# The second attention's output product in split parts, handed over group by group, without the two stops around it

## The chip, the cores and the metric

The kernel runs on one core of one Trainium2 chip. The metric is device time in microseconds (us), the median of the runs; lower is better. Five engines work side by side and meet only at semaphores: TensorE (PE, matrix products; PEld its weight loads), VectorE (DVE), ScalarE (ACT), GpSimd (POOL) and SyncE (SP, which here only issues transfers). Each engine works its own queue strictly in order, so an instruction that waits holds up all that is queued behind it on that engine.

## What is computed

A macaron transformer block (FFN, a hybrid mixer with a recurrence and a windowed attention, FFN), then two layers of a second block. Layer 1, the last, is the one that matters here:

```python
def window_attention(hl, hc, w_qkv, q_g, k_g, sink, w_o, need_ctx_out):
    ...
    ob = lax.map(block, jnp.arange(n_blocks))
    yl = jnp.moveaxis(ob, 0, 1).reshape(B, L, Q_DIM) @ w_o
    ...
        xl = xl + g1_l * yl
        hl2 = modulate(rms_norm_2(xl, norm_ffn_g[layer]), sh2_l, sc2_l).reshape(B * L, D)
        ...
        if last:
            xl = xl + g2_l * hier_moe(hl2, *moe_args).reshape(B, L, D)
```

There are 512 tokens, 1024 features, 16 query heads of 64 over 4 key heads, query blocks of 128 that see the neighbouring blocks, 256 context tokens and a sink, and a layer of 32 experts with two chosen for each token.

## The kernel before

Everything is held transposed: features on the partitions (8 tiles `k` of 128), tokens along the row. The work is one hand-written program for each engine, and what sets the order around the change is the order in which each queue was written, with semaphores between them.

**The attention loop.** Layer 1's attention has 32 units `U` (a pair of heads by a block of 128 queries), eight groups `G` of four. Unit `U` passes: scores on PE (`att_scores`, lines 705 and 710), scaling, mask and row minimum on DVE (`att_stats`, lines 1807 to 1815; `s_evac` says that the scores' banks are free, `max_ready` that the minimum is there), exponentials on ACT (`att_exps`, line 1264), transposes on PE (`att_turns`, line 726) into banks 4 and 5, and copies out of them on ACT (`att_copies`, line 1277). The engines run a few units apart: in step `U` PE turns unit `U - 2` and then scores unit `U`; ACT copies unit `U - 2` and then takes the exponentials of unit `U - 1`; DVE has the stats of unit `U`. A unit has four key blocks in the first and last quarter of the loop, five in between.

Once in four steps comes a group's end: reciprocals of the sums on DVE (`att_recips`, line 1820), turned into rows and spread over the partitions by PE (`att_rows`, `att_spread`, lines 736 and 743), the values product on PE (`att_values`, line 758), the spread reciprocals copied by ACT (`att_spread`, line 1290, into `tmp`, announced by `rec_copied`), and last `att_outputs` on DVE (line 1827), which multiplies the product by them into `f` (the tile `ar_f`) and announces `o_evac`. In DVE's step of `U % 4 == 3` the stats of unit `U` stand ahead of `att_outputs` of group `U // 4 - 1`.

**The output product.** `dense("wo", ...)` (line 535) multiplies plain f32 weights with `f`, eight tiles of eight products; the chip does each f32 product in two passes, so the trace counts 128 of them. DVE adds each tile, times a gate, to the stream `lat` (`gated_add`, lines 2232 and 2234). The weights come in four chunks of 1 MB, two tiles each, into `slot[0]` and `slot[1]`; SP loads chunks 2 and 3 when tiles 1 and 3 are done.

**The stops.** `Phase.end` drains an engine and makes it wait until all four compute engines stand there too. One stop lies between the attention and the product, one between the product and the norm.

**The norm.** ACT squares the eight tiles of `lat` (`squares`, line 1127), PE sums them over the partitions with a matrix of ones (`norm_sum`, line 680, 16 passes), ACT takes the root (`std`, line 1158), DVE inverts and scales, and `moe_layer(1)` begins: routing, then the loop over the blocks of the experts, whose weights SP streams.

**Split products.** Elsewhere the kernel already uses `split_products` (lines 547 and 553): weight and input each as a high part rounded to fp32r and a low part that is the rest, and of the four products the three that count, each one pass. ACT makes a weight piece's high part (`high`, line 1179), DVE or POOL its low part (line 1644 on DVE).

## Time and profile before

| | us |
|---|---|
| median of 3 runs | 3299.66 |
| lowest, highest | 3296.21, 3300.25 |
| the profiled execution | 3297.93 |
| its span, first to last instruction | 3296.1 |
| mean granted TensorE clock, share of full | 0.926 |
| PE, DVE, ACT, POOL busy over the span | 2822.9, 1287.4, 803.2, 365.7 |

All times in the rows are from the profiled execution, counted from its first instruction. A PE row's duration runs to the end that the profile models, and passes overlap, so the pace of the products is read from the distance between starts.

### The profile page before, as it was taken

The page shows a single profiled execution, that of the slowest core. Times are in us where ns is not written, and L with a number is a line of the kernel's source. Part 1 is how long each engine was busy: PE and PEld are TensorE (multiplying, and loading weights), DVE is VectorE, ACT ScalarE, POOL GpSimd, SP SyncE. Part 2 cuts the span into 40 slices and gives each one's busy share as a digit, 9 for nine tenths or more (in the row PEclk, how much of TensorE's full clock was granted, in tenths as well). Part 3 has the DMA queues.
Part 4 walks back from the last instruction along what each step waited for, and adds up shares of the span by engine and source line. Part 5 has one row for each costly group of instructions (what it writes and reads, how often), then busy time and mean ns, then how long its engine had stood idle before and what let it go on. Part 6 is the DMA issues. An engine that isn't in the chain of part 4 may idle for free. (4 is left out here: it accounts for less than half of the span.)

```text
span 3296.1 us, 34963 instructions
## 1 busy us (share of the span) xinstructions
PE 2822.9 (86%) x12512; PEld 1821.9 (55%) x12512; DVE 1287.4 (39%) x1978; ACT 803.2 (24%) x1338; POOL 365.7 (11%) x484
## 2 busy tenths in 40 slices
PE   6999998999989998698868888885778887888886
PEld 4888766767868886585643333333554434333332
DVE  4776576454476765303221111113386422111112
ACT  3323235454332332222210000001326520000000
POOL 0111000000000111322101111111400001111110
PEclk9999989999999999799869989897789997999998
DMA  4666521112335665110428999995110044999997
GB/s 166 211 222 219 202 69 73 64 64 78 108 128 197 213 229 187 49 64 13 169 99 346 397 401 398 403 400 235 40 37 1 1 193 187 405 402 398 402 403 286
DMA packets 117476, 672.10 MB, mean 204 GB/s; under 512 B 16398, under 2 KB 20878, under 8 KB 51856
## 3 DMA queue, kind: packets, MB, share of 16 engines
q1 hardware_dynamic: 77456, 542.63, 42.5%
q0 software_dynamic: 33600, 104.90, 9.3%
q10 hardware_dynamic: 6336, 23.50, 1.9%
q8 instruction: 47, 0.77, 0.1%
q14 instruction: 37, 0.30, 0.0%
HBM read 685.37 MB, written 24.38 MB: 215 GB/s over the span
## 5 line engine op out<-in xcount | busy, mean ns | idle before, releaser
L841 PE MATMUL bank<-big 128*64 128x512 f32 x1008 | 471.0, 613 | 102.5 <-DMA big<-in_w 100.8
L844 PE MATMUL bank<-big 128*64 128x512 f32 x1008 | 473.1, 615 | 0.0
L1983 DVE TENSOR_TENSOR big<-big,bank 64x512 f32<-64x512 f32 x65 | 44.9, 691 | 905.9 <-ACT big L1325 905.9
L841 PEld LDWEIGHTS bank<-big 128*64 128x64 f32 x1008 | 135.4, 141 | 407.8 <-issue 405.6
L856 PE MATMUL bank<-big 128*64 128x512 f32 x1008 | 269.2, 683 | 43.1 <-DVE big L1987 43.1
L1691 DVE SCALAR_TENSOR_TENSOR tabs<-tabs,tmp 128x1024 f32<-128x1024 f32 x160 | 193.3, 1222 | 182.4 <-DMA tabs<-in_wm 182.2
L2346 POOL DMA_DIRECT2D tabs<-in_wm x160 | 84.7, 530 | 1196.1 <-DVE tabs L1691 755.9
L547 PE MATMUL bank<-act_low 128*128 128x512 f32 (+1 forms) x480 | 166.6, 363 | 48.5 <-POOL u_split L2331 25.5
L1179 ACT ACTIVATE w_high<-slot 128x1024 fp32r<-128x1024 f32 (+1 forms) x134 | 136.5, 1040 | 228.3 <-DMA slot<-in_w 101.4
L856 PEld LDWEIGHTS bank<-big 128*64 128x64 f32 x1008 | 78.4, 155 | 186.9 <-issue 185.5
L1325 ACT ACTIVATE big<-bank 64x512 f32<-64x512 f32 x65 | 38.3, 589 | 537.1 <-PE bank L841 537.1
L553 PE MATMUL bank<-u_split,w_low 128*128 128x512 f32 x656 | 162.3, 389 | 3.6 <-DVE w_low L1644 3.6
L952 PE MATMUL bank<-u_split,w_high 128*128 128x512 f32 x400 | 158.8, 397 | 0.0
L952 PE MATMUL bank<-u_low,w_high 128*128 128x512 f32 x368 | 155.4, 422 | 0.2 <-ACT w_high L1179 0.2
L1331 ACT ACTIVATE big<-bank 128x512 f32<-128x512 f32 x65 | 38.8, 597 | 449.0 <-PE bank L856 449.0
L553 PEld LDWEIGHTS bank<-u_split,w_low 128*128 128x128 f32 x656 | 123.0, 188 | 29.9 <-DVE w_low L1644 4.4
L844 PEld LDWEIGHTS bank<-big 128*64 128x64 f32 x1008 | 135.2, 141 | 0.0
L547 PE MATMUL bank<-u_split,w_high 128*128 128x512 f32 x320 | 127.3, 398 | 8.2 <-ACT w_high L1179 8.2
L547 PEld LDWEIGHTS bank<-act_low 128*128 128x128 f32 x480 | 93.8, 195 | 70.5 <-issue 24.3
L547 PE MATMUL bank<-u_split 128*128 128x512 f32 x336 | 131.6, 392 | 0.0
L547 PE MATMUL bank<-u_low,u_split 128*128 128x512 f32 x336 | 130.7, 389 | 0.0
L547 PE MATMUL bank<-u_low,w_high 128*128 128x512 f32 x320 | 126.7, 396 | 0.0
(361 smaller groups left out, 5240.4 us busy)
## 6 DMA issues: line engine op xcount, KB each, us to landing
big<-in_w SPq DMA_DIRECT2D x390, 1024.0 KB
slot<-in_w SPq DMA_DIRECT2D x108, 1024.0 KB, 4.9
tabs<-in_wm POOLq DMA_DIRECT2D x160, 512.0 KB, 4.9
slot<-in_wd SPq DMA_DIRECT2D x16, 1408.0 KB, 7.1
big<-yb ACTq DMA_DIRECT2D x20, 512.0 KB, 4.8
ar_f<-in_w SPq DMA_DIRECT2D x8, 1024.0 KB
rows<-big ACTq DMA_DIRECT2D x10, 512.0 KB, 2.6
tabs<-in_w SPq DMA_DIRECT2D x4, 1024.0 KB
```

The costliest lines, as they stand in the source:

```text
L547: mm = nc.tensor.matmul(out, piece[0][k], part_of[k], start=flag, stop=False)
L553: mm = nc.tensor.matmul(out, piece[1][k], high[k], start=False, stop=(last and k == n - 1))
L841: ga = nc.tensor.matmul(bank[0][lo, :], xT[:, 4 * c + k, :], w1[:, k * EF:(k + 1) * EF], **flags)
L844: mm = nc.tensor.matmul(bank[0][hi, :], xT[:, 4 * c + k, :], w3[:, k * EF:(k + 1) * EF], **flags)
L856: mm = nc.tensor.matmul(bank[4][half, :], hT[:, 2 * c + k, :], w2[:, k * D + n * 512:k * D + (n + 1) * 512], start=(c == 0 and k == 0), st ...
L952: mm = nc.tensor.matmul(out, wh[n // 2], (lo, hi)[n % 2][n // 2], start=(n == 0), stop=False)
L1179: nc.scalar.activation(rings[ring][:, 0:at.stop - at.start], slot[s][:, at], ACT.Copy).then_inc(wh_ready, 1)
L1325: nc.scalar.activation(hsil[MB:2 * MB, :], bank[0][0:MB, :], ACT.Silu).then_inc(q["sg_ready"], 1)
L1331: nc.scalar.activation(ysb, bank[4][:, :], ACT.Copy).then_inc(q["y_ready"], 1)
L1691: nc.vector.scalar_tensor_tensor(mslot[m % 2], mslot[m % 2], 1.0, crow, ALU.mult, ALU.mult, accum_out=modf[:, idx:idx + 1]).then_inc(mod_d ...
L1983: nc.vector.tensor_tensor(hmul[MB:2 * MB, :], hsil[MB:2 * MB, :], bank[0][MB:2 * MB, :], ALU.mult).then_inc(q["h_ready"], 1)
L2346: pool.dma_start(mslot[m % 2], d["wm"][(MOD_OF[1] + MOD_OF[2])[m] // 2]).then_inc(mod_load[m % 2], 16)
```

## The change

- The output product is made of split parts: `dense` goes, and eight unrolled tiles of `split_products` (24 passes each) take its place on PE. `out_ready` lets the first four `k` of the first tile start when the groups 0 to 6 are split, the rest when group 7 is.
- `wo_high` and `wo_low` split the eight weight pieces. ACT makes the first four high parts in its attention steps 4, 8, 12 and 16, DVE their low parts in its steps 32 and 33; pieces 4 to 7 follow behind tiles 1 and 3 on both.
- `att2_split` splits each group of the attention's output: the high part on ACT in its steps 8, 12, ... 36, the low part on DVE in its steps 9, 13, ... 37.
- On DVE, `att_outputs` now stands ahead of `att_stats` in its step, where it stood behind it.
- Both stops go. The squares follow each tile on ACT into a buffer `sq_out`, DVE adds up seven of them, and PE sums two tiles (4 passes) in place of eight.
- SP's first six expert loads wait for the last values product in place of the stop; the second six for the last tile of the output product.

```diff
@@ -393,6 +397,8 @@
 
         R_MIX, W_MIX = plan["mixer"][0], PIECES_BEFORE["mixer"]
         ATT_STEPS = 3 * (UNITS + 3)
+        R_WO, L_WO, W_WO = plan["wo"][0], plan["wo"][1], PIECES_BEFORE["wo"]
+        SPLIT_HI, SPLIT_LO = 6 * KT, 3 * KT + KT // 2
 
         def done(t):
 
...
@@ -474,10 +480,14 @@
                     for c in ORDER[4:]:
                         load(c, e)
 
-                sp.wait_ge(phase_done, 4 * (3, 8)[l])
+                if l == 0:
+                    sp.wait_ge(phase_done, 4 * 3)
+                else:
+                    sp.wait_ge(o_full, 2 * (UNITS // 4))
                 for c in ORDER:
                     load(c, 0)
-                sp.wait_ge(phase_done, 4 * (3, 9)[l])
+                if l == 1:
+                    sp.wait_ge(full[3], R_WO + 2)
                 for c in ORDER:
                     load(c, 1, side=True)
...
@@ -1107,10 +1100,21 @@
                 if U > 4 and U % 4 == 2:
                     att_values(True, U // 4 - 1)
                     att_spread(True, U // 4 - 1)
-            phase.end()
-            dense("wo", 2, lambda j, k: f[:, k, :])
-            phase.end()
-            norm_sum(u2)
+
+            def out_ready(k):
+                pe.wait_ge(mx_ready, SPLIT_LO + (KT - 1 if k < 4 else KT))
+
+            for T in range(KT):
+                s, at = piece_at(T)
+                pe.wait_ge(free[T % 4], R_WO + T // 4)
+                pe.wait_ge(wl_ready, W_WO + T + 1)
+                split_products(bank[T % 4][:, :], (tiles_of(hi_ring[T % 4], KT), tiles_of(w_low[s][:, at], KT)),
+                               *([v[:, k, :] for k in range(KT)] for v in (u_low, u_high)), out_ready if T == 0 else None,
+                               True, True).then_inc(full[T % 4], 1)
+            pe.wait_ge(acc_ready, 4)
+            nc.tensor.matmul(bank[4][:, :], ones, sq_out[:, 0, :], start=True, stop=False)
+            pe.wait_ge(sq_ready, KT * norms[0] + KT)
+            nc.tensor.matmul(bank[4][:, :], ones, sq_out[:, KT - 1, :], start=False, stop=True).then_inc(ssum_ready, 1)
             moe_layer(1)
 
 
...
@@ -1276,6 +1280,18 @@
                     act.wait_ge(t_full, at + 1)
                     nc.scalar.activation(pT[:, 4 * g:4 * g + w, U % 4, :], bank[4 + at % 2][:, 0:w * P].rearrange("p (b q) -> p b q", b=w),
                                          ACT.Copy).then_inc(t_evac, 1)
+
+            def wo_high(p):
+
+                s, at = piece_at(p)
+                high(s, at, p % 4, 16 * (L_WO + p // 4 + 1), W_WO + p - 3 - 2 if p > 3 else None, hi_ring)
+
+            def att2_split(G):
+
+                x, n = unit(True, 4 * G)[:2]
+                at = slice(n * P, (n + 1) * P)
+                act.wait_ge(o_evac, UNITS // 4 + G + 1)
+                nc.scalar.activation(u_high[:, x:x + 4, at], f[:, x:x + 4, at], ACT.Copy).then_inc(mh_ready, 1)
 
             def att_rows(second, G):
                 N = (UNITS // 4 if second else 0) + G
...
@@ -1606,7 +1622,7 @@
                 nc.scalar.activation(tmp[:, 2 + x % 2, 0:n], bank[4][:, 0:n], ACT.Sqrt, bias=const("eps"),
                                      scale=1.0 / HD).then_inc(qstd_ready, 1)
             phase.end()
-            for U in range(UNITS + 4):
+            for U in range(UNITS + 5):
                 if 0 <= U - 2 < UNITS:
                     att_copies(True, U - 2, (0, 1))
...
@@ -1617,9 +1633,16 @@
                     att_rows(True, U // 4 - 1)
                 if U > 4 and U % 4 == 3:
                     att_spread(True, U // 4 - 1)
-            phase.end()
-            phase.end()
-            squares(lat[:, :, :], u2)
+                if U > 3 and U % 4 == 0 and U // 4 - 1 < 4:
+                    wo_high(U // 4 - 1)
+                if U > 7 and U % 4 == 0:
+                    att2_split(U // 4 - 2)
+            for T in range(KT):
+                act.wait_ge(free[T % 4], R_WO + T // 4 + 1)
+                nc.scalar.activation(sq_out[:, T, :], lat[:, T, :], ACT.Square).then_inc(sq_ready, 1)
+                if T % 2 and T < 4:
+                    wo_high(T + 3)
+                    wo_high(T + 4)
             std()
             moe_layer(1)
 
...
@@ -1826,6 +1849,20 @@
                 dve.wait_ge(rec_copied, 2 * N + 2)
                 nc.vector.tensor_tensor((f if second else qk1)[:, x:x + 4, n * P:(n + 1) * P], bank[6][:, :].rearrange("p (i q) -> p i q", i=4),
                                         rec2 if second else rec1, ALU.mult).then_inc(o_evac, 1)
+
+            def wo_low(p):
+
+                s, at = piece_at(p)
+                dve.wait_ge(wh_ready, W_WO + p + 1)
+                nc.vector.tensor_tensor(w_low[s][:, at], slot[s][:, at], hi_ring[p % 4].bitcast(F32), ALU.subtract).then_inc(wl_ready, 1)
+
+            def att2_split(G):
+
+                x, n = unit(True, 4 * G)[:2]
+                at = slice(n * P, (n + 1) * P)
+                dve.wait_ge(mh_ready, SPLIT_HI + G + 1)
+                nc.vector.tensor_tensor(u_low[:, x:x + 4, at], f[:, x:x + 4, at], u_high[:, x:x + 4, at].bitcast(F32),
+                                        ALU.subtract).then_inc(mx_ready, 1)
 
             def rope(src, cos, sin, count0):
...
@@ -2259,16 +2293,31 @@
             phase.end()
             nc.vector.tensor_scalar(minus_sinks, vec("sinks2"), -1.0, None, ALU.mult)
             dve.drain()
-            for U in range(UNITS + 4):
+            for U in range(UNITS + 6):
+                if U > 6 and U % 4 == 3:
+                    att_outputs(True, U // 4 - 1)
                 if U < UNITS:
                     att_stats(True, U)
+                if UNITS <= U < UNITS + 2:
+                    wo_low(2 * (U - UNITS))
+                    wo_low(2 * (U - UNITS) + 1)
                 if U > 0 and U % 4 == 0 and U <= UNITS:
                     att_recips(True, U // 4 - 1)
-                if U > 4 and U % 4 == 3:
-                    att_outputs(True, U // 4 - 1)
-            phase.end()
-            gated_add("wo", 1, 2, False)
-            phase.end()
+                if U > 8 and U % 4 == 1:
+                    att2_split(U // 4 - 2)
+            for T in range(KT):
+                dve.wait_ge(full[T % 4], R_WO + T // 4 + 1)
+                nc.vector.scalar_tensor_tensor(lat[:, T, :], bank[T % 4][:, :], mod[:, 1, 2, T, 0:1], lat[:, T, :], ALU.mult,
+                                               ALU.add).then_inc(free[T % 4], 1)
+                if T % 2 and T < 4:
+                    wo_low(T + 3)
+                    wo_low(T + 4)
+                if 1 < T:
+                    dve.wait_ge(sq_ready, 3 * KT + T)
+                    if T > 2:
+                        dve.drain()
+                    x = nc.vector.tensor_tensor(sq_out[:, 0, :], sq_out[:, 0, :], sq_out[:, T - 1, :], ALU.add)
+            x.then_inc(acc_ready, 1)
             mod_norm(1, 1, False)
             moe_layer(1)
...
@@ -2365,8 +2414,6 @@
                     low(1 if j < 2 else 0, halves[j % 2], j % 2, w0 + j + 3 + i * 4, even_ring)
             for h in range(2):
                 low(1, halves[h], h, w0 + KT + 3 + h, even_ring)
-            phase.end()
-            phase.end()
             phase.end()
             moe_layer(1)
 
```

Where the change moves instructions, three places:

**VectorE, the last two steps of the loop.** Lines 1807 to 1815 (1830 to 1838 after) are one unit's stats, 1827 (1850) is `att_outputs`, 1820 (1843) `att_recips`, 1857 `wo_low`, 1864 `att2_split`. Before:

```order
L1807 COPY big<-small 128x2 [waits s_full]
L1808 SCALAR_TENSOR_TENSOR big<-bank2_3,consts 128x2x256
L1811 TENSOR_SCALAR big<-bank0_1 128x2x256
L1815 TENSOR_REDUCE small<-big 128x2
L1807 COPY big<-small 128x2 [waits s_full]
L1808 SCALAR_TENSOR_TENSOR big<-bank2_3,consts 128x2x256
L1811 TENSOR_SCALAR big<-bank0_1 128x2x256
L1815 TENSOR_REDUCE small<-big 128x2
L1827 TENSOR_TENSOR ar_f<-bank6,tmp 128x4x128 [waits rec_copied,o_full]
L1820 RECIPROCAL rs<-rs 128x8 [waits exp_ready]
L1827 TENSOR_TENSOR ar_f<-bank6,tmp 128x4x128 [waits rec_copied,o_full]
```

Now:

```order
L1850 TENSOR_TENSOR ar_f<-bank6,tmp 128x4x128 [waits rec_copied,o_full]
L1830 COPY big<-small 128x2 [waits s_full]
L1831 SCALAR_TENSOR_TENSOR big<-bank2_3,consts 128x2x256
L1834 TENSOR_SCALAR big<-bank0_1 128x2x256
L1838 TENSOR_REDUCE small<-big 128x2
L1857 TENSOR_TENSOR w_low0<-slot0,w_high 128x1024 [waits wh_ready] x2
L1843 RECIPROCAL rs<-rs 128x8 [waits exp_ready]
L1857 TENSOR_TENSOR w_low1<-slot1,u_split 128x1024 [waits wh_ready] x2
L1864 TENSOR_TENSOR u_low<-ar_f,u_split 128x4x128 [waits mh_ready]
L1850 TENSOR_TENSOR ar_f<-bank6,tmp 128x4x128 [waits rec_copied,o_full]
L1864 TENSOR_TENSOR u_low<-ar_f,u_split 128x4x128 [waits mh_ready]
```

The output of group 6, with its waits for the copied reciprocals and the values product, moved from behind the stats of unit 31 to ahead of them; the same happened at units 7, 11, 15, 19, 23 and 27. Four weight splits follow the last stats, and a low split follows each output.

**ScalarE at the third group.** Lines 1264 (1268 after) are exponentials of one unit, 1277 (1281) copies, 1290 (1306) the spread reciprocals, 1183 `wo_high`, 1294 `att2_split`. Before:

```order
L1264 ACTIVATE big,rs<-big,small 128x641 [waits max_ready]
L1264 ACTIVATE big,rs<-big,small 128x641
L1277 ACTIVATE big<-bank5 128x2x128 [waits t_full]
L1290 ACTIVATE tmp<-bank7 128x512 [waits o_evac,rec_full]
L1277 ACTIVATE big<-bank4 128x4x128 [waits t_full]
L1277 ACTIVATE big<-bank5 128x4x128 [waits t_full]
L1264 ACTIVATE big,rs<-big,small 128x641 [waits max_ready]
L1264 ACTIVATE big,rs<-big,small 128x641
```

Now, from the same exponentials on:

```order
L1268 ACTIVATE big,rs<-big,small 128x641 [waits max_ready]
L1268 ACTIVATE big,rs<-big,small 128x641
L1281 ACTIVATE big<-bank4 128x2x128 [waits t_full]
L1183 ACTIVATE u_split<-slot1 128x1024 [waits wload1]
L1294 ACTIVATE u_split<-ar_f 128x4x128 [waits o_evac]
L1281 ACTIVATE big<-bank5 128x4x128 [waits t_full]
L1281 ACTIVATE big<-bank4 128x4x128 [waits t_full]
L1268 ACTIVATE big,rs<-big,small 128x641 [waits max_ready]
L1268 ACTIVATE big,rs<-big,small 128x641
```

Between the exponentials of one unit and the four-block copies of its transposes there now stand a weight split and a split of the second group's output.

**TensorE, from the last values product on.** Line 758 (751 after) is the values product, 743 (736) the spread. Before:

```order
L758 MATMUL bank6<-big 64x512 [waits o_evac,t_evac]
L758 MATMUL bank6<-big 64x512 x7
L743 MATMUL bank7<-rs,consts 128x128 [waits rec_copied]
L743 MATMUL bank7<-rs,consts 128x128 x3
L526 UNCONDITIONAL_BRANCH [waits phase_done]
L526 ISA
L531 REGISTER_ALU [waits wload0]
L535 MATMUL bank0_1<-ar_f,slot0 128x512 [waits free0]
L535 MATMUL bank0_1<-ar_f,slot0 128x512 x7
```

Now:

```order
L751 MATMUL bank6<-big 64x512 [waits o_evac,t_evac]
L751 MATMUL bank6<-big 64x512 x7
L736 MATMUL bank7<-rs,consts 128x128 [waits rec_copied]
L736 MATMUL bank7<-rs,consts 128x128 x3
L540 MATMUL bank0_1<-u_split,w_high 128x512 [waits mx_ready,wl_ready,free0]
L540 MATMUL bank0_1<-u_low,w_high 128x512
L540 MATMUL bank0_1<-u_split,w_high 128x512 [waits mx_ready]
```

The stop's wait is gone; in its place the first product waits for the split parts (`mx_ready`) and the first weight piece (`wl_ready`).

## Rows read from the trace of the kernel before

**Rows 1.** By stage: us; PE, PEld, DVE, ACT, POOL busy; PEclk; DMA share, GB/s.
```profile
2560.00:2617.00 57.00, 46.66 (x298) 27.42 (x298) 38.23 (x58) 38.89 (x92) 0.00 (x0) 1.00 0.00 1
2628.00:2684.00 56.00, 55.20 (x128) 24.24 (x128) 6.58 (x16) 0.00 (x0) 0.00 (x0) 1.00 0.38 150
```

**Rows 2.** Timeline at hand-over of the sixth group: start, us, engine, line, [idle before].
```profile
2597.06 0.17 DVE L1807 COPY big<-small 128x2 f32<-128x2 f32 x1 [4.94 <-PE bank L710]
...
2598.19 0.60 ACT L1290 ACTIVATE tmp<-bank 128x512 f32<-128x512 f32 x1 [0.15 <-issue]
2598.51 1.22 DVE L1815 TENSOR_REDUCE small<-big 128x2 f32<-128x1026 f32 x1
...
2599.65 0.68 DVE L1827 TENSOR_TENSOR ar_f<-bank,tmp 128x512 f32<-128x512 f32 x1
2599.77 0.72 ACT L1264 ACTIVATE big<-big,small 128x513 f32<-128x513 f32 x1
...
2601.36 1.09 PE L726 MATMUL bank<-consts,big 128*128 128x128 f32 x8 [1.10 <-ACTq L1266]
2602.05 1.08 ACT L1277 ACTIVATE big<-bank 128x512 f32<-128x512 f32 x2 [0.77 <-PE bank L726]
```

**Rows 3.** Timeline at the second group's hand-over, where a unit has five blocks.
```profile
2520.70 0.17 DVE L1807 COPY big<-small 128x2 f32<-128x2 f32 x1 [4.13 <-PE bank L710]
...
2522.06 0.59 ACT L1290 ACTIVATE tmp<-bank 128x512 f32<-128x512 f32 x1
...
2523.94 0.83 ACT L1264 ACTIVATE big<-big,small 128x641 f32<-128x641 f32 x1 [0.31 <-DVE small L1815]
...
2526.44 1.08 ACT L1277 ACTIVATE big<-bank 128x512 f32<-128x512 f32 x2 [0.28 <-PE bank L726]
```

**Rows 4.** Weight splits: ScalarE's high part and VectorE's low part of one piece.
```profile
L1179 ACT ACTIVATE w_high<-slot 128x1024 fp32r<-128x1024 f32 (+1 forms) x134 | 136.5, 1040 | 228.3 <-DMA slot<-in_w 101.4
...
L1644 DVE TENSOR_TENSOR w_low<-slot,u_split 128x1024 fp32r<-128x1024 f32 (+1 forms) x68 | 78.4, 1190 | 27.4 <-ACT u_split L1179 27.4
```

**Rows 5.** Granted clock around the end of the attention: us, PE busy, PEclk, DMA.
```profile
2614.00:2617.00 3.00, 1.09 (x8) 0.93 0.03 5
2617.00:2620.00 3.00, 2.12 (x10) 0.50 0.00 0
```

**Rows 6.** Timeline of TensorE and VectorE from the seventh values to the output product.
```profile
2606.70 3.65 PE L758 MATMUL bank<-big 128*64 128x512 f32 x16
...
2617.88 1.97 PE L726 MATMUL bank<-consts,big 128*128 128x128 f32 x8 [2.16 <-ACTq L1266]
...
2620.54 5.05 PE L758 MATMUL bank<-big 128*64 128x512 f32 x16 [0.16 <-ACT big L1277]
...
2627.41 0.69 DVE L1827 TENSOR_TENSOR ar_f<-bank,tmp 128x512 f32<-128x512 f32 x1 [9.34 <-ACT tmp L1290]
...
2628.47 55.20 PE L535 MATMUL bank<-ar_f,slot 128*128 128x512 f32 x128 [1.80 <-POOLq L358]
```

**Rows 7.** Timeline of a split product in layer 1's q: the first pass of two tiles.
```profile
2366.16 0.39 PE L547 MATMUL bank<-act_low 128*128 128x512 f32 x1
...
2371.60 0.39 PE L547 MATMUL bank<-act_low 128*128 128x512 f32 x1
```

**Rows 8.** Timeline of the norm behind the output product.
```profile
2684.99 4.27 ACT L1127 ACTIVATE ar_u<-lat 128x512 f32<-128x512 f32 x8 [57.69 <-DVEq L358]
...
2685.77 7.10 PE L680 MATMUL bank<-ar_u,consts 128*128 128x512 f32 x16 [2.10 <-ACT ar_u L1127]
...
2689.28 1.28 ACT L1158 ACT_TABLE_LOAD   x1
...
2692.91 0.69 ACT L1158 ACTIVATE rs<-bank,consts 128x512 f32<-128x512 f32 x1 [2.35 <-PE bank L680]
```

**Rows 9.** The routing weights' transfer in both layers (line 1294).
```profile
L1294 ACTq DMA_DIRECT2D big<-in_wr x2: 339/342/345, 1634.7 to 2692.9; - x2
...
DMA to landing us min/median/max: 7.3/7.5/7.6
```

29 lines of the change are left out of this document (7 added, 22 removed).

## The prediction

> **What bounds the kernel now.** I read the table by stage first [rows 1]. Before the output product lies the attention loop, in which no engine is full (PE 46.7 of 57 us, ACT 38.9, DVE 38.2, almost no DMA), so what counts there is the order in which the queues meet. The product itself is PE alone, 55.2 of 56 us at full clock. Then I read the timeline at a group's hand-over, because the change puts new work into every one [rows 2]. Unit 27's stats start at 2597.06, the row minimum runs from 2598.51 to 2599.73, and the exponentials of unit 27 start at 2599.77, 0.04 behind it; `att_outputs` stands behind the minimum at 2599.65. Behind the exponentials PE waits 1.10 us for ACT's drain, and ACT then waits 0.77 us for PE's transposes. So minimum, exponentials, transposes, next scores and next minimum are one chain, and ACT's own chain runs level with it. In the five-block units the exponentials even wait 0.31 us for the minimum, and ACT's gap before its copies is only 0.28 us [rows 3]. Last I read the norm behind the product [rows 8], which is serial.
>
> **The product (a gain).** Plain f32 now takes 55.20 us for 128 passes, from 2628.47 to 2683.67 [rows 6]. A split tile of 24 passes takes 2371.60 - 2366.16 = 5.44 us at full clock [rows 7]. TensorE ends the last spread at about 2626.7 and can at once start the half of the first tile that needs only groups 0 to 6. The other half needs group 7: its output ends at 2627.41 + 0.69 = 2628.10, its high part on ACT costs some 0.60 (a copy of that size, [rows 2]), its low part on DVE some 0.69, with hand-overs 2629.5. From there 16 passes (3.6) and seven tiles (38.1) give 2671.2, against 2683.67: **12.5 us gained**, the first stop included. The cover of the other pieces: chunks 2 and 3 are asked for at the end of tiles 1 and 3 and needed two tiles, 10.9 us, later; from that go two high parts of 1.04 and a low part of 1.19 [rows 4], which leaves some 7.6 us for a transfer of 1 MB. The first four weight splits on DVE (4 x 1.19) lie behind the last stats, under the last exponentials, transposes and values product (to 2625.6, [rows 6]).
>
> **The norm (a gain).** From the last product to the root it takes 2692.91 - 2683.67 = 9.24 us now: the gated add, the stop, eight squares with 16 passes (7.10 us, 0.44 a pass) [rows 6, 8]. After: gated add 0.7, the last sum of squares on DVE 0.7, four passes 1.8, pipeline and hand-overs 0.4: 3.6 us. The last square (4.27/8 = 0.53) and the table load (1.28) run beside the sum and the passes and end earlier, 2.6 us after the product [rows 8]. **5.6 us gained.** If DVE's weight splits were late, this would grow; they are done four tiles before.
>
> **The output ahead of the stats (a loss).** This line of the diff looks like tidying, and it is the largest term. `att_outputs` waits for ACT's copy of the spread reciprocals. At unit 27 that copy runs from 2598.19 to 2598.79 [rows 2]; ahead of the stats, the output runs to about 2599.5, and the stats start there, not at 2597.06: 2.4 us late. Queued behind the waiting output on DVE are the stats; for them wait the exponentials (0.04 us of slack) and, by `s_evac`, PE's next scores. Nothing later in the group gives it back: the next exponentials, transposes and scores each follow from this one, and the values product of the next group from those. With five blocks: the copy ends at 2522.65, the output at 2523.3, the stats started at 2520.70: 2.6 us [rows 3]. Seven hand-overs have stats behind them (units 7, 27 and 31 with four blocks, 11, 15, 19 and 23 with five): 3 x 2.4 + 4 x 2.6 = **17.6 us lost**.
>
> **ACT's new work (a loss).** It stands in steps 4, 8, ... 28 between exponentials and copies, where ACT now idles 0.77 us (four blocks) or 0.28 (five) [rows 2, 3]. A weight piece costs 1.04 [rows 4], a group's high part 0.60. Step 4: 1.04 - 0.77 = 0.3. Step 8: 1.64 - 0.77 = 0.9. Steps 12 and 16: 1.64 - 0.28 = 1.4 each. Steps 20 and 24: 0.60 - 0.28 = 0.3 each. Step 28: covered. **4.5 us lost.** DVE's low parts (0.69 in a step) lie in gaps of about that size in front of the next scores; I take them at nothing, at most 0.2 each.
>
> **The clock (a loss of unsettled size).** The one place in the loop's last 60 us where the clock fell is its end: PE turned unit 30 and then waited 2.16 us; it had worked 1.09 of 3 us, and the next stretch ran at 0.50, that is at 1.2 GHz [rows 5, 6]. The transposes of unit 31 took 1.97 us where those at full clock took 1.09, and the values product 5.05 where it takes 3.65 [rows 2, 6]. After the change every hand-over looks like that: PE has the transposes of unit 26 (1.09), waits some 1.7 us for the late scores' banks, scores for about 1.1, and waits 1.7 again for the late exponentials. A fall there costs one unit's transposes (0.9) and, at the same ratio, its scores (an estimate of 1.0 to 1.1), so about 2 us; if it lasts into the values product, 1.4 more. From below: no fall, 0. From above: seven falls of 3.4, 24 us. PE's work in these stretches is close to that of the one row which fell, but each hand-over meets the chip's looking at another moment, so I take four falls of seven: **8 us lost**.
>
> **Behind the norm: nothing.** SP's second six loads start at the last tile instead of 8 us before the root, so the routing weights' transfer stands among them earlier in their course. It lands after 7.3 and 7.6 us in the two layers [rows 9], though in layer 0 twelve loads are issued ahead of it and here six; its time does not hang on the backlog. Routing and the loop of experts then start with the root and move with it.
>
> **The sum**, against the profiled execution's 3297.93: -12.5 - 5.6 + 17.6 + 4.5 + 8 = +12 us, so 3309.9; the median lies 1.7 above that execution, and by it the forecast is **3312 us**.
>
> **The rivals.** (1) *The clock holds.* All terms but the clock's: +4 us, 3304. For it: the clock stayed at 1.00 over the whole stretch of [rows 1] with PE busy 82%. Against it: the hand-overs are to have far less work than that mean. (2) *The clock falls at every hand-over* and mostly reaches the values product: 7 x 3.1 = 22 in place of 8, +26, 3326. For it: the one like stretch fell. Against it: the fall at the end came with the longest single wait, 2.16 us, and the new ones are 1.7. The Trainium skill (TensorE: Matmul & The Clock Gate, Part 4: PE-mode transpose) says that work in transpose mode does not count as busy for the clock in the way that products do; by it the hand-overs, where transposes are half of the work, would all fall, and the sum would be this rival's. The trace does not bear it out so far: the stretch of [rows 1] holds transposes in every unit and shows 1.00. (3) *The stats' delay is absorbed* (the faster end). If the group's chain has slack that I do not see, say because the values product of 3.65 us on PE and not the stats sets the group's length, the 17.6 goes and with it the clock's term: -12.5 - 5.6 + 4.5 = -13.6, 3286. It decides from the point where less than about 11 of the 17.6 us arrives. Against it: the exponentials follow the minimum within 0.04 us [rows 2] or wait for it [rows 3], and the values product comes behind the scores that this delays. (4) *The change doesn't do what it says*: the first half of the first tile does not run ahead, or the second chunk's splits come late behind tile 3. The first is worth 1.8 us, the second up to a tile, 5 us more.
>
> **How the numbers follow.** Chances: the forecast (two to six falls) 0.42, (1) 0.24, (2) 0.12, (3) 0.12, other sizes of the same terms, (4) among them, 0.10. 0.2% is 6.6 us, about what a measurement can tell from no change. Slower by more: 0.40 of the forecast, 0.02 of (1), all of (2), 0.04 of the rest: 0.58. Within: 0.02 of the forecast, 0.22 of (1), 0.03: 0.27. Faster: (3) and 0.03: 0.15. The range leaves out (3) and the upper half of (2): from 3295 to 3324.
>
> **What would show it.** Right: seven times DVE's stats of units 7 to 31 start behind `att_outputs`, some 2.4 us later against the scores' end than now; the loop from its first scores to the last spread is 22 us longer without falls, 30 with; PEclk rows under 1.00 inside the loop; eight product tiles 5.44 us apart; 3.6 us from the last product to the root. Wrong: exponentials of units 7, 11, ... that do not wait for DVE, or a loop that is less than 15 us longer; then (3) is the case, and the kernel is faster.

## The result, and the profile after

The changed kernel takes 3302.77 us (median of 20 runs, 3295.25 to 3307.75), the kernel before 3297.02 in the same comparison (20 runs). The ratio is 1.0018, with a 95% interval of 1.0011 to 1.0025: slower by 5.75 us. The profiled execution's span went from 3296.1 to 3301.5 us. That is inside the range and on the side of the forecast, but less than half of its size: +12 was forecast, +5.75 came by the medians and +5.4 in the profiled span.

First the place that was to lose most. This is the timeline at the second group's hand-over in the kernel after, which answers to [rows 3] (start, us, engine, line; in brackets the idle time before and what ended it):

```profile
2525.10 0.59 ACT L1306 ACTIVATE tmp<-bank 128x512 f32<-128x512 f32 x1
...
2525.79 0.69 DVE L1850 TENSOR_TENSOR ar_f<-bank,tmp 128x512 f32<-128x512 f32 x1 [5.57 <-ACT tmp L1306]
2526.40 0.16 DVE L1830 COPY big<-small 128x2 f32<-128x2 f32 x1
...
2528.07 0.92 PE L698 MATMUL bank<-big 64*128 64x384 f32 x4 [2.16 <-DVE big L1834]
...
2529.63 0.83 ACT L1268 ACTIVATE big<-big,small 128x641 f32<-128x641 f32 x1 [2.96 <-DVE small L1838]
...
2531.44 1.12 PE L719 MATMUL bank<-consts,big 128*128 128x128 f32 x8 [1.65 <-ACTq L1270]
```

VectorE waits 5.57 us for ScalarE's copy of the reciprocals, makes the output, and only then starts the stats. The exponentials, which waited 0.31 us for the minimum before [rows 3], now wait 2.96: 2.65 more. TensorE's two waits are 2.16 us ahead of the scores and 1.65 ahead of the transposes; the forecast took 1.7 for both, and counted it against rival 2 that no new wait was as long as the 2.16 of the loop's end. At every one of the seven hand-overs they came 2.42 (four blocks) or 2.65 us (five) later, 17.85 together.

The clock in two such stretches (us from the span's start; length, busy us of PE, PEld, DVE, ACT, POOL; then PEclk, DMA share, GB/s), behind the first hand-over and behind the second:

```profile
2502.00:2505.00 3.00, 1.58 (x14) 0.94 (x10) 0.63 (x2) 2.83 (x8) 0.00 (x0) 1.00 0.00 0
2505.00:2508.00 3.00, 1.62 (x6) 1.02 (x8) 2.54 (x5) 0.69 (x2) 0.00 (x0) 0.64 0.00 0
2508.00:2511.00 3.00, 2.62 (x14) 1.73 (x10) 1.98 (x4) 2.90 (x7) 0.00 (x0) 0.50 0.00 0
...
2526.00:2529.00 3.00, 0.93 (x6) 0.68 (x8) 2.91 (x5) 0.67 (x2) 0.00 (x0) 1.00 0.00 0
2529.00:2532.00 3.00, 1.35 (x11) 0.74 (x10) 2.91 (x5) 2.27 (x6) 0.00 (x0) 1.00 0.00 0
```

It fell to 0.50 behind five of the seven hand-overs (units 7, 15, 19, 23 and 27). Behind that of unit 11, the second stretch here, it did not, and that of unit 31 runs into the fall at the loop's end, which was there before [rows 5].

Then the product's start and its pace, which answer to [rows 6, 7]:

```profile
2644.38 4.34 PE L751 MATMUL bank<-big 128*64 128x512 f32 x16 [0.16 <-ACT big L1281]
...
2649.74 0.50 PE L540 MATMUL bank<-u_split,w_high 128*128 128x512 f32 x1
...
2652.68 0.50 PE L540 MATMUL bank<-u_split,w_high 128*128 128x512 f32 x1 [0.84 <-DVE u_low L1864]
...
2656.48 0.39 PE L540 MATMUL bank<-u_split,w_high 128*128 128x512 f32 x1
```

Eight passes run ahead behind the last spread, then PE waits 0.84 us for the last group's low part, as foretold. From the second tile's start at 2656.48 on, the tiles are 5.44 us apart, and VectorE's last gated add starts at 2694.76. More passes take less time here because each is shorter: 5.44/24 = 0.23 us in split parts, 55.20/128 = 0.43 us in plain f32, where a tile of 16 took 6.9 [rows 6, 7]. The norm behind it, against [rows 8]:

```profile
2694.76 0.75 DVE L2310 SCALAR_TENSOR_TENSOR lat<-bank,mod,lat 128x512 f32<-128x512 f32 x1 [3.90 <-PE bank L546]
...
2695.55 0.63 ACT L1642 ACTIVATE big<-lat 128x512 f32<-128x512 f32 x1 [4.80 <-DVE lat L2310]
...
2696.19 1.28 ACT L1162 ACT_TABLE_LOAD   x1
2696.35 1.12 PE L1115 MATMUL bank<-big,consts 128*128 128x512 f32 x2 [1.62 <-DVE big L2319]
...
2697.31 1.02 PE L1117 MATMUL bank<-big,consts 128*128 128x512 f32 x2
...
2698.37 0.69 ACT L1162 ACTIVATE rs<-bank,consts 128x512 f32<-128x512 f32 x1 [0.90 <-PE bank L1117]
```

The root starts 3.61 us behind the last gated add, where it took 8.75 (that gated add started at 2684.16 in the kernel before, the root at 2692.91 [rows 8]). From the root to the span's end it is 603.1 us now and 603.2 before, so nothing behind the norm changed.

### The profile page after: what moved, and what is told of

It is laid out like the page before. It is cut to its first block and busy times, and to the rows that moved or that the text cites. A ratio compares the mean times of both kernels' runs of the same rounds, so it can differ in the third digit from the quotient of the medians.

```text
span 3301.5 us, 35062 instructions
## 1 busy us (share of the span) xinstructions
PE 2816.7 (85%) x12564; PEld 1838.9 (56%) x12564; DVE 1303.5 (39%) x1992; ACT 816.6 (25%) x1354; POOL 365.8 (11%) x484
## 5 line engine op out<-in xcount | busy, mean ns | idle before, releaser
L546 PE MATMUL bank<-u_split,w_low 128*128 128x512 f32 x720 | 178.1, 389 | 4.0 <-DVE w_low L1667 4.0
L945 PE MATMUL bank<-u_split,w_high 128*128 128x512 f32 x400 | 158.2, 396 | 0.0
L945 PE MATMUL bank<-u_low,w_high 128*128 128x512 f32 x368 | 154.8, 421 | 0.2 <-ACT w_high L1183 0.2
L546 PEld LDWEIGHTS bank<-u_split,w_low 128*128 128x128 f32 x720 | 135.0, 188 | 32.9 <-DVE w_low L1667 4.9
L540 PE MATMUL bank<-u_split,w_high 128*128 128x512 f32 x352 | 139.2, 395 | 9.0 <-ACT w_high L1183 8.2
L540 PE MATMUL bank<-u_split 128*128 128x512 f32 x368 | 144.0, 391 | 0.0
L540 PE MATMUL bank<-u_low,u_split 128*128 128x512 f32 x368 | 143.2, 389 | 0.0
L540 PE MATMUL bank<-u_low,w_high 128*128 128x512 f32 x352 | 138.4, 393 | 0.0
```

The costliest lines, as they stand in the source:

```text
L540: mm = nc.tensor.matmul(out, piece[0][k], part_of[k], start=flag, stop=False)
L546: mm = nc.tensor.matmul(out, piece[1][k], high[k], start=False, stop=(last and k == n - 1))
L945: mm = nc.tensor.matmul(out, wh[n // 2], (lo, hi)[n % 2][n // 2], start=(n == 0), stop=False)
```

## Experiments

**How the runs are read.** In every trace I took the start of each unit's first exponential, less the start of the first unit's stats, and subtracted the same for the kernel before. What is left is how late a unit is by what happened inside the loop. Two of the ends of this, for the kernels before and after (first stats, and the first exponential of unit 31):

```profile
2472.98 0.17 DVE L1807 COPY big<-small 128x2 f32<-128x2 f32 x1 [1.91 <-PE bank L710]
...
2616.29 0.72 ACT L1264 ACTIVATE big<-big,small 128x513 f32<-128x513 f32 x1
```

```profile
2473.15 0.17 DVE L1830 COPY big<-small 128x2 f32<-128x2 f32 x1 [1.91 <-PE bank L703]
...
2640.13 0.72 ACT L1268 ACTIVATE big<-big,small 128x513 f32<-128x513 f32 x1 [2.30 <-DVE small L1838]
```

So unit 31 is (2640.13 - 2473.15) - (2616.29 - 2472.98) = 23.67 us late. Lateness in us of the units ahead of a hand-over and at it (7, 11, ... are at one); the last column is the root's, counted in the same way:

| kernel | 6 | 7 | 10 | 11 | 14 | 15 | 18 | 19 | 22 | 23 | 26 | 27 | 30 | 31 | root |
|---|---|---|---|---|---|---|---|---|---|---|---|---|---|---|---|
| after | -0.06 | 2.36 | 2.87 | 5.52 | 6.35 | 9.00 | 9.83 | 12.47 | 13.59 | 16.24 | 17.80 | 20.22 | 21.25 | 23.67 | 5.29 |
| order back (e1_order) | -0.12 | -0.11 | -0.06 | -0.06 | 0.78 | 0.78 | 1.61 | 1.61 | 1.60 | 1.60 | 1.71 | 1.72 | 1.71 | 1.72 | -16.01 |
| output ahead alone (e2_ahead) | -0.01 | 2.41 | 1.76 | 4.41 | 5.78 | 8.43 | 9.96 | 12.61 | 12.36 | 15.01 | 16.31 | 18.73 | 19.61 | 22.03 | 24.63 |
| ScalarE's work moved (e4_idle) | 0.02 | 2.44 | 2.95 | 5.60 | 7.09 | 9.74 | 9.49 | 12.14 | 13.29 | 15.93 | 17.48 | 19.91 | 20.96 | 23.38 | 4.97 |
| filler of three (e8_short) | -0.09 | 2.34 | 2.39 | 5.04 | 5.87 | 8.52 | 9.34 | 11.99 | 11.86 | 14.51 | 14.62 | 17.05 | 17.05 | 19.47 | 0.99 |

My theory after the result (theory B in the expectations): the seven hand-overs cost what was forecast, 17.9 us, but ScalarE's new work and the clock together cost only 6, and not 12.5, since they stand beside slack and beside each other. The rival (A) was the forecast's own: each term has its full size, and something else gave back some 6 us. The letters of the rivals change from one expectation to the next; each says what its own stand for.

### The order put back

```diff
             for U in range(UNITS + 6):
-                if U > 6 and U % 4 == 3:
-                    att_outputs(True, U // 4 - 1)
                 if U < UNITS:
                     att_stats(True, U)
 ...
                     att_recips(True, U // 4 - 1)
+                if U > 6 and U % 4 == 3:
+                    att_outputs(True, U // 4 - 1)
```

> The changed kernel with one thing undone: VectorE's output of a group stands behind the stats of its step again, as before the change. Theory (the order is the loss): the seven hand-overs give back 17.9 us (3 x 2.42 + 4 x 2.65 in the trace of the changed kernel), the clock stays at full in the loop, and of the 6.0 us between the hand-overs some 3 stay for ScalarE's new work; so 18 to 21 us faster than the changed kernel, 13 to 16 faster than before. Rival A (the splits inside the loop are the loss, the order is innocent): no faster than the changed kernel, within 3 us.

Measured: 3284.04 us, ratio to the kernel before 0.9961 (0.9947 to 0.9975); again on another chip 3281.18, ratio 0.9953 (0.9937 to 0.9970). This kernel is faster than both. No hand-over makes a unit late, the clock is 1.00 from unit 2 to unit 30, and the root is 21.3 us nearer to the loop's start than in the kernel after (-16.01 against 5.29). So one line's place on VectorE costs 21 us by the traces (17.85 directly, 4.1 by the clock in the loop, less 0.7 at its end) and 19 to 21 by the ratios of the two comparisons.

What is left in the loop is ScalarE's work alone: 0.28 us at step 4, 0.06 at 8, 0.83 at 12, 0.83 at 16 and 0.11 at 24, 2.1 together; units 2 and 3 came 0.4 earlier than in the kernel before, so that 1.7 is left at unit 31. That 0.4 is scatter between executions and no part of the change: two kernels below that differ only from unit 31 on have -0.3 there and 0.0. ScalarE at steps 8 and 12 in this kernel:

```profile
2505.06 1.06 ACT L1183 ACTIVATE w_high<-slot 128x1024 fp32r<-128x1024 f32 x1
...
2506.03 0.61 ACT L1294 ACTIVATE u_split<-ar_f 128x512 fp32r<-128x512 f32 x1
...
2506.55 1.06 ACT L1281 ACTIVATE big<-bank 128x512 f32<-128x512 f32 x2
...
2524.14 0.38 ACT L1281 ACTIVATE big<-bank 128x256 f32<-128x256 f32 x1
2524.42 1.05 ACT L1183 ACTIVATE u_split<-slot 128x1024 fp32r<-128x1024 f32 x1
2525.37 0.62 ACT L1294 ACTIVATE u_split<-ar_f 128x512 fp32r<-128x512 f32 x1
2525.89 1.07 ACT L1281 ACTIVATE big<-bank 128x512 f32<-128x512 f32 x2
2526.84 0.84 ACT L1268 ACTIVATE big<-big,small 128x641 f32<-128x641 f32 x1
```

The same two places in the kernel before:

```profile
2507.43 1.09 ACT L1277 ACTIVATE big<-bank 128x512 f32<-128x512 f32 x2 [0.77 <-PE bank L726]
2509.13 0.83 ACT L1264 ACTIVATE big<-big,small 128x641 f32<-128x641 f32 x1 [0.62 <-DVE small L1815]
...
2525.77 0.39 ACT L1277 ACTIVATE big<-bank 128x256 f32<-128x256 f32 x1
...
2527.65 0.83 ACT L1264 ACTIVATE big<-big,small 128x641 f32<-128x641 f32 x1
```

Both pieces hold the queue from 2505.06 to 2506.55, 1.49 us and not 1.64, since each instruction here starts about 0.09 us before the one ahead of it ends by the profile. At step 8, 0.77 of it lies in the gap ahead of the copies and 0.62 in the wait that the next exponentials had anyway: 0.10 is left. At step 12 it is 1.47 (2524.42 to 2525.89); the copies followed the short one at 0.67 us before [rows 3] and follow it at 0.28 with nothing between, which covers 0.39, and the exponentials that came 1.21 behind the copies' start come 0.95 behind it now, 0.26. That leaves 0.82, and 0.83 was measured.

### The output ahead, alone

The kernel before, with its output in front:

```diff
             for U in range(UNITS + 4):
+                if U > 4 and U % 4 == 3:
+                    att_outputs(True, U // 4 - 1)
                 if U < UNITS:
                     att_stats(True, U)
                 if U > 0 and U % 4 == 0 and U <= UNITS:
                     att_recips(True, U // 4 - 1)
-                if U > 4 and U % 4 == 3:
-                    att_outputs(True, U // 4 - 1)
```

> The kernel before with one thing changed: VectorE's output of a group stands ahead of the stats of its step. Theory: 17.9 us slower by the seven hand-overs, plus what the clock's falls cost alone, 3 to 7 us, since ScalarE has no new work here: 21 to 25 us slower than before. Rival A: within 3 us of before.

Measured: 3324.74 us, ratio 1.0085 (1.0071 to 1.0099), 27 us slower than before by the medians, more than expected, and 24.6 by its trace's root. The hand-overs again cost 2.42 to 2.65 us each. Between them the units grow later by 4.2 us in sum, with none of ScalarE's work there: by 1.37, 1.53, 1.30 and 0.88 behind units 11, 15, 23 and 27, where the clock fell each time, and by -0.65 and -0.25 behind 7 and 19, where it did not. The stretch behind unit 11:

```profile
2520.00:2523.00 3.00, 1.93 (x10) 0.97 (x10) 2.83 (x5) 0.37 (x1) 0.00 (x0) 0.85 0.00 0
2523.00:2526.00 3.00, 1.81 (x10) 1.57 (x8) 2.89 (x4) 2.16 (x6) 0.00 (x0) 0.50 0.00 0
```

So the order alone brings the falls: the four groups with one lost 5.1 us. The 0.65 and 0.25 are part of the hand-over's delay given back. Before, the exponentials of unit 8 waited 0.62 us for their minimum (the row at 2509.13 above); here they don't:

```profile
2505.18 0.83 ACT L1264 ACTIVATE big<-big,small 128x641 f32<-128x641 f32 x1
```

The stats of unit 8 now start 2.79 us behind those of unit 7 and not 3.46, since TensorE has turned unit 6 in its wait and scores unit 8 at once. The root is 24.6 us late, 2.6 more than unit 31: the end of the loop took 0.8 less, the product began at a lower clock (58.46 us from the last output to the last gated add, 56.75 before), and the norm took 10.43 us in place of 8.75, since the clock fell there too:

```profile
2703.00:2706.00 3.00, 3.00 (x4) 1.44 (x5) 0.00 (x0) 3.00 (x7) 0.00 (x0) 0.50 0.90 281
```

### ScalarE's work moved

The kernel after, with the weight pieces' high parts and the groups' splits in the steps in which ScalarE and VectorE wait for the values product:

```diff
-                if U > 3 and U % 4 == 0 and U // 4 - 1 < 4:
+                if U > 4 and U % 4 == 2 and U // 4 - 1 < 4:
                     wo_high(U // 4 - 1)
-                if U > 7 and U % 4 == 0:
+                if U > 8 and U % 4 == 2 or U == UNITS + 4:
                     att2_split(U // 4 - 2)
 ...
-                if U > 8 and U % 4 == 1:
+                if U > 8 and U % 4 == 2 or U == UNITS + 5:
                     att2_split(U // 4 - 2)
```

> The changed kernel with the new splits inside the loop moved on both engines to the step in which the values product holds them up anyway (ScalarE idles 3.9 us there, VectorE 4.1): weight pieces, high parts and low parts all two or one step later. The output stays ahead of the stats. Theory B: the falls of the clock stay and now show in every group, so of the 6.0 us between hand-overs 5 or more stay: 0 to 1.5 us faster than the changed kernel. Rival D (it is ScalarE's work): 5 to 6 us faster.

Measured: 3305.07 us, ratio 1.0028 (1.0016 to 1.0040): nothing gained, and unit 31 is 23.38 us late against 23.67. ScalarE's work costs nothing in these steps, as the kernel with the order put back as well shows (below), but here the clock's falls take its place. The stretches behind the first hand-over:

```profile
2502.00:2505.00 3.00, 1.85 (x6) 1.18 (x8) 2.32 (x3) 0.69 (x2) 0.00 (x0) 0.55 0.00 0
2505.00:2508.00 3.00, 2.62 (x14) 1.63 (x10) 2.21 (x4) 1.56 (x5) 0.00 (x0) 0.50 0.00 0
2508.00:2511.00 3.00, 2.41 (x13) 1.32 (x13) 2.13 (x5) 2.33 (x5) 0.00 (x0) 0.82 0.00 0
```

The clock now fell behind 7, 11, 19, 23 and 27. Behind 11, with no other work on ScalarE, units 12 to 14 lost 1.49 us, where the kernel after lost 0.83 to ScalarE's work with no fall.

### A filler in the waits: what the clock costs

PE multiplies constants into the bank of the spread reciprocals, ahead of the scores of a hand-over and ahead of the next step's transposes, where it waits in the kernel after. Nothing reads these products. First six in each place:

```diff
+            def keep_busy(n, G):
+                pe.wait_ge(rec_copied, 2 * (UNITS // 4 + G) + 2)
+                for _ in range(n):
+                    nc.tensor.matmul(bank[7][:, 0:2 * P], ident, consts[:, 0:2 * P], start=True, stop=True)
+
             for U in range(UNITS + 3):
+                if U > 8 and U % 4 == 1:
+                    keep_busy(6, U // 4 - 2)
                 if 0 <= U - 2 < UNITS:
                     att_turns(True, U - 2, (0, 1))
+                if U > 7 and U % 4 == 0:
+                    keep_busy(6, U // 4 - 2)
                 if U < UNITS:
                     att_scores(True, U)
```

> The kernel after with six products of 256 columns that nothing reads (on the bank of the spread reciprocals) ahead of the scores in the steps of hand-over, and ahead of the transposes in the step behind them, so that PE works in its two waits (1.65 and 2.16 us) there. Only the clock is to change. Theory A (the prediction's term: four or five falls at 2 us each, beside the rest): 8 us faster than the kernel after, some 3295. Theory B (the falls lie beside ScalarE's late work and are partly given back at the values product, and are worth 4 us together): 3 to 5 us faster than the kernel after, 3298 to 3300, and the hand-overs' 17.9 us stay. Rival C: the products themselves come in the way (1.3 us in a wait of 1.1 to 1.7), and the kernel is as slow as the kernel after or slower. Left out: nothing of the result.

Measured: 3298.94 us, ratio 1.0006 (0.9997 to 1.0015): 4 us faster than the kernel after by the ratios, 0.6 by the root of its trace (4.67 late). The clock was 1.00 in the whole loop, and yet unit 31 was 24.24 us late: rival C had part of it, since six products took 2.8 us, longer than the waits, and the transposes came late behind them. That run could not settle the price, so the filler was halved:

```diff
-                    keep_busy(6, U // 4 - 2)
+                    keep_busy(3, U // 4 - 2)
```

> The run with the filler again, with three products of 256 columns in each of the two places and not six. Six took 2.8 us in waits of 1.1 to 2.2 us: the clock stayed at 1.00 in the whole loop, but the exponentials still came 22 us late at the last unit, since PE was busy with the filler when it was wanted. Three take 1.4 us. Theory B (the clock is worth about 4 us in this loop and the rest of the 23.7 us by which unit 31 is late is the hand-overs' 17.9 and ScalarE's 1.7): clock at 1.00, exponentials of unit 31 late by 19 to 20.5 us and not 23.7, last output late by 20 or less, and a kernel 4 to 6 us faster than the kernel after, some 3297 to 3299. Theory A (each fall costs 2 us beside the rest): unit 31 late by 14 to 16 us, the kernel 8 or more us faster. Rival: with less work in them the waits let the clock fall again, and nothing is gained.

Measured: 3295.56 us, ratio 1.0001 (0.9992 to 1.0010), where the kernel after has 1.0018: 5.6 us faster. TensorE behind the first hand-over, and the clock there:

```profile
2499.75 1.46 PE L1095 MATMUL bank<-consts 128*128 128x256 f32 x6
2501.61 0.92 PE L698 MATMUL bank<-big 64*128 64x384 f32 x4 [0.40 <-DVE big L1844]
...
2502.89 1.56 PE L1095 MATMUL bank<-consts 128*128 128x256 f32 x6
```

```profile
2502.00:2505.00 3.00, 2.95 (x19) 1.94 (x16) 2.77 (x5) 2.00 (x5) 0.00 (x0) 1.00 0.00 0
2505.00:2508.00 3.00, 2.19 (x16) 1.14 (x14) 2.40 (x5) 3.00 (x7) 0.00 (x0) 1.00 0.00 0
```

PE still waits 0.40 us for the stats, so the filler does not reach past that wait, and the clock holds as far as unit 31. Behind unit 31, where both fillers stand in one wait, 2.76 us of products followed by 1.99 of waiting, it fell all the same:

```profile
2634.00:2637.00 3.00, 2.58 (x8) 0.77 (x8) 2.37 (x3) 0.70 (x3) 0.00 (x0) 0.53 0.00 0
```

Unit 31 is 19.47 us late, the root 0.99. Against the kernel after (23.67 and 5.29) the clock's price in the loop is 4.2 us, for five falls. Group by group, the lateness that arises between two hand-overs, after against this run:

| behind unit | 7 | 11 | 15 | 19 | 23 | 27 | sum |
|---|---|---|---|---|---|---|---|
| after | 0.51 | 0.83 | 0.83 | 1.12 | 1.56 | 1.03 | 5.88 |
| filler of three | 0.05 | 0.83 | 0.82 | -0.13 | 0.11 | 0.00 | 1.68 |
| the fall's share | 0.46 | none fell | 0.01 | 1.25 | 1.45 | 1.03 | 4.2 |

### Both put right

The order back, and ScalarE's work moved (the two diffs above together).

> The kernel after with two edits: att_outputs stands behind the stats again on DVE, and ScalarE's new work (a high part of the output weights, a high part of a group's output) with the low part on DVE stands in the steps of a group in which those engines wait for the values product, as in the run that moved it alone. Theory B (what the loop loses is set by where the work meets the chain, and with the order put back the clock does not fall, so that ScalarE's work has a price of its own, 1.7 us in the run with the order alone put back): 1.5 to 2 us faster than that run, 3280 to 3283 where the kernel before takes 3297, ratio 0.995. Rival A (ScalarE's work in these steps brings a fall of the clock or a wait of its own, as it gained nothing where the output stood ahead): the same as that run or slower, ratio 0.996 to 0.997.

Measured: 3276.64 us, ratio 0.9932 (0.9918 to 0.9945). From unit 2 to unit 31 the units stay 0.3 us early, the scatter named above, and nothing is added, so ScalarE's work is free where it stands now. The two ratios of this kernel and of the one with the order alone had been taken on different chips and stood 9 us apart, their traces 2.2. So both ran once more side by side.

> The order put back and ScalarE's work moved, again. By the traces (loop 2.0 us shorter than in the run with the order alone, last output 3.0 us earlier) it should be 2 to 3 us faster than that one on the same chip, ratio 0.9945 to 0.9955. Rival: the 9 us of the two chips' ratios are real, and there is something in the rest of the kernel that this version gains.

> The kernel after with the order of att_outputs and the stats put back alone, timed again beside the next one on one chip. The two were timed on different chips, at ratios of 0.9961 and 0.9932 to the kernel before, which is 9 us apart where their traces are 2.2 us apart. Expected here: 0.995 to 0.996.

Measured: 3279.67 us, ratio 0.9944 (0.9927 to 0.9960), beside 3281.18 and 0.9953 for the order alone. The difference is 1.5 us by the medians and 2 to 3 by the traces. The 9 us did not come again; with five runs of each on different chips, what made them is not shown.

### The old stops and the old norm

The kernel with both put right, with the stops behind the loop and the product, eight squares, their 16 passes and the old waits of SP's loads restored, so that the split product stands alone (the edit on PE):

```diff
+            phase.end()
             for T in range(KT):
                 s, at = piece_at(T)
 ...
-            pe.wait_ge(acc_ready, 4)
-            nc.tensor.matmul(bank[4][:, :], ones, sq_out[:, 0, :], start=True, stop=False)
-            pe.wait_ge(sq_ready, KT * norms[0] + KT)
-            nc.tensor.matmul(bank[4][:, :], ones, sq_out[:, KT - 1, :], start=False, stop=True).then_inc(ssum_ready, 1)
+            phase.end()
+            norm_sum(u2)
```

> The kernel of the other run (order back, work moved) with the stop behind the loop, the stop behind the product, and the old norm: eight squares and 16 passes behind the stop. So the split product stands alone. By the prediction's terms it loses against that run 5.6 us for the norm and 1.8 us for the head start of the first half of the first tile: 7.4 us slower, ratio against the kernel before 0.997 to 0.998. Rival: the last gated add and the squares do not set the root (something else late there, as the weights' low parts), and the difference is under 4 us.

Measured: 3285.57 us, ratio 0.9959 (0.9945 to 0.9972), 8.9 us slower than the kernel without them. Both ends of the product:

```profile
2629.61 0.57 PE L540 MATMUL bank<-u_split,w_high 128*128 128x512 f32 x1 [2.91 <-DVEq L362]
...
2675.09 0.75 DVE L2311 SCALAR_TENSOR_TENSOR lat<-bank,mod,lat 128x512 f32<-128x512 f32 x1 [4.69 <-PE bank L546]
...
2683.83 0.69 ACT L1162 ACTIVATE rs<-bank,consts 128x512 f32<-128x512 f32 x1 [2.35 <-PE bank L673]
```

The norm takes 8.74 us from the last gated add, where it takes 3.61 in the kernel after: 5.1 us. The other 3.5 lie at the product's start: the wait for the stop, 2.91 us, loses the head start of 1.8, and the clock was low behind it, so that the first nine passes started some 0.42 us apart and not 0.23. From the last output to the last gated add it is 47.66 us, so of the 12.5 gained in the kernel after, 9.1 are the split product's alone (56.75 before) and 3.5 the stop's.

### A filler at the loop's end

The kernel with both put right, with filler products between the transposes of unit 30 and those of unit 31, first eight and then four:

```diff
             for U in range(UNITS + 3):
+                if U == UNITS + 1:
+                    keep_busy(8, U // 4 - 2)
```

> The kernel with the order put back and ScalarE's work moved, with eight products of 256 columns that nothing reads between the transposes of unit 30 and those of unit 31, where PE waits 2.16 us and the clock then falls in all kernels so far: transposes 1.97 us where they take 1.09, values product 5.03 where it takes 3.65. Theory A (a fall costs what its instructions take longer, when nothing beside it gives it back): the clock stays at 1.00 there, and the kernel is 2.0 to 2.5 us faster than the one without these products. Rival: the products reach past the wait, or the clock falls all the same: no difference or slower by up to 1 us.

Measured: 3277.69 us, ratio 0.9945 (0.9932 to 0.9959): no difference to the kernel without them. The clock stayed at 1.00, but eight products took 3.6 us in a wait of 2.2. Four:

> The kernel with the order put back, ScalarE's work moved and a filler at the end of the loop, with four products of 256 columns there and not eight. Eight took 3.6 us in a wait of 2.2 and so delayed unit 31's transposes by 1.1 us, but the clock stayed at 1.00 and the values product took 3.65 us. Four take 1.8 us and fit. Expected: transposes of unit 31 at once behind their exponentials, clock at 1.00, first product of the output some 1.2 us nearer to the loop's start than with eight and 2 us nearer than without filler; the kernel 1.5 to 2.5 us faster than the same without filler. Rival: four are too few and the clock falls as before, no difference.

TensorE at the loop's end with four products:

```profile
2611.93 1.09 PE L719 MATMUL bank<-consts,big 128*128 128x128 f32 x8 [1.10 <-ACTq L1278]
2612.86 1.89 PE L1095 MATMUL bank<-consts 128*128 128x256 f32 x8
2615.19 1.09 PE L719 MATMUL bank<-consts,big 128*128 128x128 f32 x8 [0.43 <-ACTq L1278]
...
2617.02 3.65 PE L751 MATMUL bank<-big 128*64 128x512 f32 x16
```

And without filler, in the kernel with both put right (its second run):

```profile
2618.55 1.28 PE L719 MATMUL bank<-consts,big 128*128 128x128 f32 x8 [2.16 <-ACTq L1270]
...
2620.52 4.74 PE L751 MATMUL bank<-big 128*64 128x512 f32 x16
```

The transposes of unit 31 take 1.09 us and the values product 3.65, where they took 1.97 and 5.05 before [rows 6]. From the first exponential of unit 31 to the last output it is 8.9 us. It was 11.1 in the kernel before and with the order alone put back, but 10.1 in the kernel that differs by the filler alone, where the fall caught less of the transposes (1.28). So a fall with nothing beside it cost 2.2 us in one case and 1.2 in the other, and the expected 2 us were 1.2. The kernel took 3276.84 us, ratio 0.9941 (0.9924 to 0.9959). By its trace it is the best of all (root 19.9 us early, against 19.0); by the measured times it cannot be told from the kernel without filler (2.8 us by the medians of one comparison).

## Why the prediction was half right

In its own terms, from the traces (us):

| term | forecast | measured | from |
|---|---|---|---|
| split product, first stop | -12.5 | -12.5 | last output to last gated add: 56.75 before, 44.21 after |
| norm, second stop | -5.6 | -5.1 | last gated add to root: 8.75, 3.61 |
| output ahead of the stats | +17.6 | +17.85 | 3 x 2.42 + 4 x 2.65 |
| ScalarE's work | +4.5 | +1.7 | unit 31 in the run with the order back: 2.1 by its steps, less the 0.4 of scatter |
| clock, in the loop | +8 | +4.1 | 23.67 - 17.85 - 1.72; 4.2 against the filler of three |
| the loop's last 11 us | 0 | -0.7 | unit 31's exponentials to the last output: 11.12, 10.42 |
| behind the norm | 0 | 0 | 603.2, 603.1 |
| sum | +12 | +5.3 | root: +5.29 |

**Right.** The line that looks like tidying was the largest term, and its size was read to 0.3 us from two hand-overs: ScalarE's copy ends at a known time, the output takes 0.7, and the stats and the exponentials behind it have no slack. The product's gain and the head start came as worked out, the norm within 0.5 us. Rival 3, that the delay is absorbed, is out: each hand-over made its unit late by the full 2.42 or 2.65 us, and unit 31 was 19.47 late even where the clock held. Rival 4 is out: the first half ran ahead, and the tiles stood 5.44 us apart.

**The step that failed is the sum of the last two terms of the loop,** ScalarE's work and the clock: 12.5 us forecast, 5.8 measured.

Of the clock the mechanism was right, and the count nearly: five falls for the four taken. The price of one fall was wrong: 2 us forecast, 0.84 on the average. The forecast built it from what the fall at the loop's end did to the transposes (0.9), and added the scores at the same ratio (1.1). That the whole fall at the loop's end costs 1.2 to 2.2 us agrees with the 2 only by chance, since no scores stand there and the values product makes up the rest. In the middle of the loop a fall has other work beside it. Behind unit 15 unit 17 was 1.2 us later than with the filler (10.25 against 9.03), and unit 18 only 0.5, which is what unit 15 already was. The rest was given back on TensorE: ahead of unit 16's transposes it waits 1.37 us for ScalarE with the filler and 0.20 in the kernel after, so that the values product starts only 0.5 later. Behind 19 and 23 a part was, and 1.25 and 1.45 stayed. The prediction's "nothing later in the group gives it back" was written of the stats' delay, and the clock's price was added in full as if it held for the transposes too, without a look for their slack. For the stats it is not quite right either: with the output ahead alone and no fall, 0.65 us came back behind unit 7 and 0.25 behind unit 19.

Of ScalarE's work, 4.5 was forecast and 1.7 measured. The forecast added durations (1.04 + 0.60) and took off one gap. The rows had two more: an instruction holds its queue for less than its duration, 1.49 for both; and the exponentials' own wait for the minimum, which the prediction names itself for five blocks (0.31, [rows 3]) and for other reasons, can hold ScalarE's work as well. At step 8 that wait is 0.62 and leaves 0.06 of a forecast 0.9. In the kernel after this slack can be used once: either the hand-over's delay gives back its 0.65 there or ScalarE's work stands in it, so the split of the sum between these two terms holds to about that much, and their total is what is measured.

The two terms are not independent either, which the run with ScalarE's work moved shows: it took that work's 2.1 us away, and the clock's falls took 5.5 in place of 4.1. Rival 1 (the clock holds, +4 us in the forecast's sum) came nearest in time, and by luck: the clock did not hold, and ScalarE's work was 2.8 us less than in that sum. Rival 2 (a fall at every hand-over, 22 us) was near in its count and not in its price: with unit 31's, six of seven hand-overs met a fall, and those that were new cost 4.1 us. The statement of the Trainium skill that it named (TensorE: Matmul & The Clock Gate, Part 4: PE-mode transpose) is that work in transpose mode does not count as busy in the same way. The traces do not show it deciding here: the loop with the order back has as many transposes and held 1.00. Whether transposes count less than products, no run here tells, since the filler added work of one kind only.

**The chances.** 3304, rival 1's time, had 0.24, and the forecast 0.42. By size, a change of 5.75 us lies within the 6.6 us to which the prediction gave 0.27, where it gave 0.58 to more. With the loop's two terms as measured the sum would have been +5 to +6. What stays open is why the clock held behind unit 11, with PE busy 0.93 and 1.35 us in two stretches of 3 (shown above), and fell behind unit 7, with 1.58: the rows don't tell it, and in the run with ScalarE's work moved it was unit 15 behind which it held.

## What to carry to other kernels

Before a line is moved ahead in an engine's queue, look up what it waits for and by how much that comes later than the start of what it is put in front of: the difference, and its own length with it (here 1.7 and 0.7 us), is the price, once per turn of the loop, and a reorder of two instructions undid here all that a faster product (12.5 us) and a shorter norm (5.1) had gained. When a delay is priced, take off every wait that its engine has between here and the next hand-over, and not the first gap alone; count what an instruction holds its queue, from start to next start. Price a fall of TensorE's clock from a place with the same neighbours, since at the end of a chain it cost 1.2 to 2.2 us and in the middle of this one 0 to 1.45.
